# The new tokens' 64-row tile multiplied in float32 with the raw weights

## The reference, cut to what matters

```python
z = gelu(h @ w_in); u, v = split(z)                    # layer 0: 1024 -> 2 x 2048, v is normed and mixed over positions
a = h @ w_in; c_q, c_kv, k_r = split(a)                # layer 1: 1024 -> 384 + 256 + 32, each part normed
q  = (c_q  @ w_uq ).reshape(S, 16, 64 + 32)            # 384 -> 16 heads x 96
kv = (c_kv @ w_ukv).reshape(S, 16, 64 + 64)            # 256 -> 16 heads x (64 key + 64 value columns)
```

## Time and profile before

| | |
|---|---|
| median of 3 runs | 1471.11 us (1470.96 to 1471.82) |
| the profiled execution | 1471.75 us, its span 1469.9 us |
| PE / PEld (weight loads) busy | 1459.4 us (99%) / 1377.7 us (94%) |
| DVE / ACT / POOL busy | 827.2 / 618.6 / 703.2 us |
| matmul records | 10556 |
| granted TensorE clock | 1.00 |
| DMA | 120.33 MB, mean 82 GB/s |

### The profile page before, as it was taken

How to read it: one execution, slowest core, us unless ns; L and a number is a source line. 1 busy time by engine, 2 the same in 40 slices (tenths; PEclk the granted TensorE clock), 3 DMA queues, 4 the chain that set the end, 5 groups by cost and what they waited for, 6 DMA issues and landing times.

```text
span 1469.9 us, 29054 instructions
## 1 busy us (share of the span) xinstructions
PE 1459.4 (99%) x10556; PEld 1377.7 (94%) x10556; DVE 827.2 (56%) x1499; ACT 618.6 (42%) x1234; POOL 703.2 (48%) x474
## 2 busy tenths in 40 slices
PE   9999999999999999999999999999999999999998
PEld 7889999999999999999997778787999999999998
DVE  6006716755654635636778676867556536356365
ACT  5323201123533434435637585766135344344352
POOL 7554455443363453543776052452433644535434
PEclk9999999999999999999999999999999999999999
DMA  7322232231133131231343110101221331312412
GB/s 236 105 83 72 77 105 80 63 86 58 47 127 101 58 114 57 86 117 55 118 152 89 30 44 15 43 18 39 77 67 44 127 95 66 114 57 86 117 56 93
DMA packets 36385, 120.33 MB, mean 82 GB/s; under 512 B 6040, under 2 KB 6744, under 8 KB 36064
## 3 DMA queue, kind: packets, MB, share of 16 engines
q1 hardware_dynamic: 31456, 109.86, 24.1%
q10 hardware_dynamic: 4864, 9.61, 2.0%
HBM read 115.91 MB, written 3.55 MB: 81 GB/s over the span
## 4 chain that ended last, share of the span: by engine, by line
PE 49%; DVE 2%; issue 1%; ACT 1%; DVEq 0%
PE ps L720 8%; PE ps L722 8%; PE ps L721 8%; PE ps L881 5%; PE ps L883 5%; PE ps L882 5%; PE ps L1159 2%; PE ps L1101 2%; PE ps L978 2%; PE ps L1112 1%; PE ps L1104 1%; PE ps L983 1%; PE ps L1026 1%; PE ps L1073 1%; DVE lat L1541 1%
## 5 line engine op out<-in xcount | busy, mean ns | idle before, releaser
L720 PE MATMUL ps<-h_hi,w_hi 128*128 128x288 f32 x1280 | 380.6, 297 | 0.0
L721 PE MATMUL ps<-h_lo,w_hi 128*128 128x288 f32 x1280 | 377.5, 295 | 0.0
L722 PE MATMUL ps<-h_hi,w_lo 128*128 128x288 f32 x1280 | 376.3, 294 | 0.0
L652 POOL TENSOR_TENSOR w_lo<-raw,w_hi 128x512 fp32r<-128x512 f32 x128 | 172.0, 1354 | 213.5 <-ACT w_hi L1879 213.3
L881 PE MATMUL ps<-op_hi,w_hi 128*128 128x288 f32 x896 | 265.5, 296 | 1.1 <-DVE x L1454 1.1
L882 PE MATMUL ps<-op_lo,w_hi 128*128 128x288 f32 x896 | 264.3, 295 | 0.0
L883 PE MATMUL ps<-op_hi,w_lo 128*128 128x288 f32 x896 | 263.4, 294 | 0.0
L722 PEld LDWEIGHTS ps<-h_hi,w_lo 128*128 128x128 f32 x1280 | 241.0, 188 | 0.0
L720 PEld LDWEIGHTS ps<-h_hi,w_hi 128*128 128x128 f32 x1280 | 239.8, 187 | 1.2
L721 PEld LDWEIGHTS ps<-h_lo,w_hi 128*128 128x128 f32 x1280 | 240.3, 188 | 0.0
L636 POOL TENSOR_TENSOR w_lo<-raw,w_hi 128x1024 fp32r<-128x1024 f32 x60 | 144.3, 2411 | 183.7 <-ACT w_hi L1871 183.7
(11 more groups left out here) (211 smaller groups left out, 2730.9 us busy)
## 6 DMA issues: line engine op xcount, KB each, us to landing
raw<-stream SPq DMA_DIRECT2D x206, 512.0 KB, 3.6
out_x<-x ACTq DMA_DIRECT2D x8, 288.0 KB, 2.5
x<-xt SPq DMA_DIRECT2D x4, 288.0 KB, 5.9
x<-xt ACTq DMA_DIRECT2D x4, 288.0 KB, 9.1
raw<-stream ACTq DMA_DIRECT2D x2, 512.0 KB, 7.0
b_bc<-bs ACTq DMA_DIRECT2D x2, 512.0 KB, 7.0
cache_raw<-cache_ct ACTq DMA_DIRECT2D x1, 1024.0 KB, 6.5
v_out<-sgu_grow ACTq DMA_DIRECT2D x1, 512.0 KB, 4.7
```

What stands on the lines that cost most here:

```text
L652: nc.gpsimd.tensor_tensor(block_of(w_lo, b), factor(i, b), block_of(w_hi, b).bitcast(F32), ALU.subtract).then_inc(split_lo, 1)
L720: nc.tensor.matmul(out, l_hi, r_hi, start=first, stop=False)
L721: nc.tensor.matmul(out, l_hi, r_lo, start=False, stop=False)
L722: return nc.tensor.matmul(out, l_lo, r_hi, start=False, stop=last)
```

## The change

Tile 4 of the gating values, the latents and the queries, and the last key tile, are multiplied in float32: one instruction with the float32 activations as stationary operand and the raw weight unit as streamed operand, in place of `three` or `packed`. The other tiles are unchanged. With it:

- `h_new` (DVE, 8 small products x times gain, one per k behind each `low_part`), `h_new2` (POOL, one product of 8 x 64 elements behind the first MLP, which waits for the last x tile and comes before the `split` loop), `cq_new` and `c_new` (ACT, one copy each in `take_latents`) hold the float32 activations of the 64 rows.
- PE waits for `first_new` in chunk 0 and for `new_set` at tile 4 of the first unit of each latent chunk.
- A raw slot is now read by PE until the unit is used, so `plain` waits for `unit_done` of the unit too before it reloads the slot, in the gating values, the latents and the head groups.
- `h_pair`, `packed`, `copy_low_half` and `fold_samples` go, with their semaphores.

```diff
-            def plain(first, end, lows):
+            def plain(first, end, lows, done=None):
+
                 for unit in range(first, end):
                     sp.wait_ge(split_lo, unit - first + lows + 1)
+                    if done is not None:
+                        sp.wait_ge(unit_done, unit - first + done + 1)
                     sp.dma_start(raw[:, unit % SLOTS, :], stream[unit]).then_inc(raw_loaded[unit % SLOTS], 16)
...
-            plain(SLOTS, U_MLP0 + SLOTS, 0)
+            plain(SLOTS, U_SGU + SLOTS, 0, 0)
+            plain(U_SGU + SLOTS, U_MLP0 + SLOTS, U_SGU)
...
-            plain(U_IN + SLOTS, U_GRP + 2 * SLOTS, L_IN)
+            plain(U_IN + SLOTS, U_GRP + SLOTS, L_IN, D_IN)
...
-            plain(U_GRP + 2 * SLOTS, U_MLP1 + SLOTS, L_IN + U_GRP + SLOTS - U_IN)
+            plain(U_GRP + SLOTS, U_O + SLOTS, L_IN + U_GRP - U_IN, D_GRP)
+            plain(U_O + SLOTS, U_MLP1 + SLOTS, L_IN + U_O - U_IN)
...
+            pool.wait_ge(gains_loaded, 16)
+            pool.wait_ge(tile_read, F_O + 2)
+            nc.gpsimd.tensor_tensor(h_new2[:], x[:, :, SEQ:T], gains_sb[:, 2, :].unsqueeze(2).broadcast_to([P, KD, DEC]),
+                                    ALU.mult).then_inc(new_set, 1)
...
-                            if pack and t == NT - 1:
-                                last = packed(ps[:, bank_of(parity, t), 0:width], k, w_hi[:, j, w], w_lo[:, j, w],
-                                              k == 0, k == KD - 1)
+                            if t == NT - 1:
+                                if chunk >= 4 and j == 0:
+                                    pe.wait_ge(new_set, 1)
+                                elif chunk == 0:
+                                    pe.wait_ge(first_new, k + 1)
+                                last = nc.tensor.matmul(ps[0:DEC, bank_of(parity, t), 0:width],
+                                                        (h_new2 if chunk >= 4 else h_new)[:, k, :], raw[:, j, w],
+                                                        start=(k == 0), stop=(k == KD - 1))
                                 continue
...
-                        for t in range(NT):
+                        for t in range(NT - 1):
                             last = nc.tensor.matmul(ps[0:ROWS[t], bank_of(0, t), 0:512], l[:, k, cols(t)], r[:, j, w],
                                                     start=(k == 0 and n == 0), stop=False)
+                    pe.wait_ge(first_new, k + 1)
+                    last = nc.tensor.matmul(ps[0:DEC, bank_of(0, NT - 1), 0:512], h_new[:, k, :], raw[:, j, w],
+                                            start=(k == 0), stop=False)
...
+                        if t == NT - 1:
+                            last = nc.tensor.matmul(ps[0:DEC, q_bank(t, first), 0:HG * QK], cq_new[:, k, :],
+                                                    raw[:, k, 0:HG * QK], start=(k == 0), stop=(k == 2))
+                            continue
...
+                        if j == KT_N - 1:
+                            last = nc.tensor.matmul(ps[0:r, key_bank(j), 0:width], c_new[:, k, :], raw[:, 3, w],
+                                                    start=(k == 0), stop=(k == 1))
+                            continue
...
+                nc.vector.tensor_scalar(h_new[:, k, :], x[:, k, SEQ:T], gains_sb[:, 0, k:k + 1], None,
+                                        ALU.mult).then_inc(first_new, 1)
...
+                    if L % NT == NT - 1:
+                        nc.scalar.copy((cq_new if L < NT else c_new)[:],
+                                       ps[:, latent_bank(L), col:col + n_k * P].rearrange(
+                                           "p (k c) -> p k c", k=n_k)[:, :, 0:r])
```

More of the change, by code:

```diff
@@ L226, in build_trunk @@
         hid_lo = place("hid_lo", [P, KD, T], F32R, b_at + 4 * KD * T)
-        h_pair = place("h_pair", [P, KD, 2 * DEC], F32R, b_at)
+        h_new = place("h_new", [P, KD, DEC], F32, b_at)
         lat = place("lat", [P, NT, QL + KL + ROPE], F32, b_at)
@@ L231, in build_trunk @@
         krr = place("krr", [P, NT, QK], F32, b_at + 4 * (NT + 1) * LAT)
+        h_new2 = place("h_new2", [P, KD, DEC], F32, b_at + 4 * (NT + 1) * LAT + 4 * NT * QK)
+        assert 4 * (NT + 1) * LAT + 4 * NT * QK + 4 * KD * DEC <= 8 * KD * T
         v_at = region(4 * NT * DS)
@@ L246, in build_trunk @@
         cqT_lo = place("cqT_lo", [P, 3, T], F32R, v_at + 16 * KEYS + 12 * T)
+        cq_new = place("cq_new", [P, 3, DEC], F32, v_at + 16 * KEYS + 24 * T)
+        c_new = place("c_new", [P, 2, DEC], F32, v_at + 16 * KEYS + 24 * T + 12 * DEC)
+        assert 16 * KEYS + 24 * T + 20 * DEC <= 4 * NT * DS and 2 * op_bytes + 32 * TH <= 8 * KD * T + 16 * KEYS + 24 * T
         s_at = region(4 * KT_N * HG * VD)
@@ L353, in build_trunk @@
         tok_read = sem_of("tok_read")
-        pair_set = sem_of("pair_set")
-        fold_set = sem_of("fold_set")
-        folded = sem_of("folded")
+        first_new = sem_of("first_new")
+        new_set = sem_of("new_set")
         v_set = sem_of("v_set")
@@ L764, in norm_spread @@
                 last.then_inc(rms_spread, 1)
[L766 to L770, removed]
             def token_chunk(chunk, parity, first_unit, width, between=None, h_count=None, tiles=None,
-                            halves_apart=False, pack=False):
+                            halves_apart=False):
                 for j in range(2 if h_count == 0 else 0, 4):
@@ L834, in _ @@
             pe.wait_ge(var_set, 2)
-            pe.wait_ge(pair_set, 2)
             def spread_first():
@@ L841, in _ @@
             for c in range(1, 4):
-                token_chunk(c, c % 2, 4 * c, 512, pack=True, between={2: spread_first} if c == 3 else None)
+                token_chunk(c, c % 2, 4 * c, 512, between={2: spread_first} if c == 3 else None)
             pe.wait_ge(rms_bc_set, 2)
@@ L1224, in norm_diagonal @@
                 last.then_inc(diag_set, 1)
[L1226 to L1229, removed]
             def clear_sums():
@@ L1286, in _ @@
             norm_diagonal(0)
-            for c in range(1, 4):
-                fold_samples(c - 1, v[0:DEC, NT - 1, c * 512:(c + 1) * 512], bank_of(c, NT - 1))
             dve.wait_ge(const_loaded, 16 * CONSTS)
@@ L1755, in _ @@
             nc.scalar.activation(junk[:, 0:1], ones[:, 0:1], ACT.Square)
-            def copy_low_half(bank, width):
-                nc.scalar.copy(mixed[0:DEC, 0:width], ps[DEC:2 * DEC, bank, 0:width]).then_inc(fold_set, 1)
             def load_half(half):
@@ L1805, in _ @@
             load_half(0)
[L1806 to L1809, removed]
             norm_root(0)
@@ L1824, in _ @@
                     vc = v[0:r, t, c * 512:(c + 1) * 512]
[L1825 to L1829, removed]
+                    nc.scalar.activation(vc, ps[0:r, bank_of(parity, t), :], ACT.Gelu,
                                          scale=rms_tok[0:r, t:t + 1]).then_inc(tok_read, 1)
```

## The result

The changed kernel takes 1508.65 us (median of 4 runs, 1506.99 to 1510.05), the kernel before 1471.36 us beside it: ratio 1.025, 95% interval 1.024 to 1.026. That is 37.3 us slower where 30.2 were predicted, and 0.65 us above the range. The profiled execution took 1510.05 us with a span of 1508.2 us, 38.3 us more than the span of before. It is the slowest of the four runs: PE's mean granted clock was 0.996 in two of them (1510.05 and 1508.4 us) and 0.998 in the other two (1508.9 and 1506.99 us).

A forecast was written before the change was run, and what follows sets the result against it. PE, busy 99% of the span, was taken as the bound. Products 15.4, change-overs 13.3 and the `new_set` stall 1.5 made 30.2 us: 1502.0 us profiled, 1501.3 by the median; range 1487 to 1508 us.

The forecast's parts named there:

- What a product costs: On PE, a 64-row float32 product costs 0.86 us at 512 columns, 0.64 at 384, 0.48 at 288.
- Reading (b): A product runs its two records in a row, 0.86 us; two products in different array halves run together.
- R1: Rival: both records of a product run at once, 0.43 us at 512 columns; +4.7 us, 1475.8 us; chance 0.12.
- R2: Rival: both records at once and change-overs hidden in the float32r stream; -8.6 us, 1462.5 us; chance 0.03.
- The change-over: On PE, each stretch of 64-column float32 products costs 0.36 us, 35 stretches; with the key tiles +13.3 us.
- R3: Rival: records in a row, but change-overs cost nothing; +15.4 + 1.5 us, 1488.0 us; chance 0.06.
- The table: Dearer products in gating, latents, queries and last key: together +15.4 us, of which gating chunks 1 to 3 +9.6.
- `first_new`: Chunk 0: DVE's eight small products before the squares are hidden by DVE's 3.03 us standing; nothing, up to 0.5 us.
- `new_set`: PE waits for POOL's `h_new2` at tile 4 of the first latent unit: 1.5 us, bounds 1.0 and 2.0.
- the waits that were filled: Head group 0: longer products may fill some 0.5 us of PE's 1.6 us stall before L1026; left in the range.
- The late reload: Units ready 7.2 us after their slot's last use, hidden by PE's three units in hand; at worst 1 us once.

The follow-up runs named there:

- e5: e2 with the two tile 4 products of a unit in gating chunks 1 to 3 written to different PSUM partition halves, then added: 1490.94 us, ratio 1.0137.
- e4: e2 with tile 4 of two units multiplied in one stretch (chunks 0 to 5), 14 change-overs fewer: 1496.07 us, ratio 1.017.
- e2: e1 with the latents' `h_new2` also made by ACT, k by k, instead of POOL's one product: 1497.58 us, ratio 1.0175.
- e1: The changed kernel with the eight `h_new` products of the start on ACT instead of DVE: 1500.93 us, ratio 1.020.
- e3: The kernel before with only the changed, later reload of the raw slots, no float32 product: 1476.21 us, ratio 1.003.
- e6: e2 with tile 4 of gating chunks 1 to 3 back to packed float32r products, with copy and fold: 1487.56 us, ratio 1.0106.
- e8: e6 with the same two waits on POOL as e7 (the hold): 1482.76 us, ratio 1.0077.
- e7: e3 with POOL held: low parts of units 19 and 123 wait for DVE's first `vn` products and its latents: 1471.48 us, ratio 1.000.

## Why the prediction was wrong, point by point

**What a product costs** was right. Reading (b), two records in a row of 0.43 us, stands in the loads of the kernel after, and e5 shows that it is the missing partner. R1 and R2 fall with it. R1 rested on a start in program order; read by (b), the pairs of the earlier trace rows are products of two heads side by side. So the second head's first product starts 0.01 us behind the first head's first (807.63 and 807.62), ahead of the first head's second (808.53), which stands before it in the program.

**The change-over** was right: 0.34 us measured directly in the kernel after, 0.34 and 0.32 by taking 14 of them away (e4), 0.36 predicted. R3 falls. The table and the change-overs were 28.7 us in the prediction; e2 has 26 us left.

**`first_new`, the step that failed.** The prediction put it so: "DVE's eight small products lie in front of the squares. DVE then stood 3.03 us waiting for PE, and PE comes to that point later still: hidden." It took the eight for nearly nothing; they took 15.4 us of DVE, 10.4 us net on the squares' start. And it took 3.03 us of standing behind the squares for slack in front of them. That was 1.7 us, and 2.8 more because PE itself came later: 10.4 - 1.7 - 2.8 = 5.9. The cost was 9.1 us of the gating by the traces of the kernel after and e1 (the stall of 5.9 and the half clock behind it are 8.8), 7.7 by the medians. Without it, e1 is 0.4 us from the forecast of 1501.3. That is partly luck: `new_set` and the reload cost more than was forecast, the waits that were filled gave more.

The trace of before had the warning. DVE and POOL of the kernel before, in order of time:

```profile
17.87 2.95 DVE L1239 SCALAR_TENSOR_TENSOR h_lo<-x,gains_sb,h_hi 128x576 fp32r<-128x576 f32 x1
...
17.43 2.78 POOL L613 TENSOR_TENSOR w_lo<-raw,w_hi 128x1024 fp32r<-128x1024 f32 x1
20.18 1.56 POOL L611 TENSOR_SCALAR w_hi<-raw 128x1024 fp32r<-128x1024 f32 x1
```

`h_lo`, which alone takes 0.8 us, takes 2.95 there and ends behind POOL's `w_lo`. POOL's next `w_hi` takes 1.56 us instead of the 1.05 of an undisturbed one. The two engines already held each other up in this stretch. An operation added to DVE there costs what is left of POOL's, however small it is itself. The Trainium skill states the rule, in SBUF — State Buffer, section Who interferes with whom: DVE and GpSimd share a port pair as an exclusive lock, and whoever issues second is blocked for the other's whole instruction, for `tensor_scalar` in a two-port mode and for DVE operations with two inputs in SBUF against GpSimd ones that read it. These traces agree (2.37 us for 64 elements, 3.35 for two `vn` products), and so does ACT's 0.33.

**`new_set`** was right in kind and place. The stall was 1.8 us in place of 1.5, since `h_new2` took 1.55 us and not 1.2. The 1.7 us of half clock behind it in the kernel after had not been counted; e1, with the same stall and no half clock, is 1.6 us shorter in the latents. e2 got 2.3 us back there, 3.35 by the medians.

**The late reload, the second step that failed.** "PE has three units in hand ... Hidden." That PE does not wait for weights was right, and e3 has no such wait. But the sum asked only whether the weights come in time, not where POOL's work goes when it is shifted, and what it falls on there: 4.5 us in e3. In the kernel after itself little of it shows: 0.8 us before L961, in head group 0, and no wait for `vn`. There the fold of tile 4 is gone, and DVE begins `vn` at 143.93, 3.2 us before PE's product that reads it (147.10) and ahead of POOL's next `w_hi` (144.68); in the kernel before it was 1.0 us (120.08 and 121.11). The wait came back in e5 and e6, which have the fold, and with 0.8 us in e4, which has not. So the late reload cost the changed kernel about 1 us (the hold gave 1.1 in e8's head groups), and stood ready for the next edit.

**The sum, redone for the kernel after:** products 15.4, 35 stretches at 0.34 and the key tiles 12.6, first stall and its clock 8.8, `new_set` and its clock 3.5, waits for `h_lo` and `lat` 1.3: 41.6 us, against 38.3 measured between the spans. By stage: gating 26.4 (26.8 measured), latents 7.8 (7.0), head groups 7.4 (6.2), feature tiles 0 (-1.2), start 0 (-0.5). Most of the gap is waits that the kernel before has and the kernel after has not. In the feature tiles and the first MLP those of before are

```profile
PE ps L881 <- DVE x L1454: 1.1, 2, 0.8
PE ps L862 <- DVE vn L1305: 0.3, 1, 0.3
```

and the kernel after waits 0.2 us for x and not for `vn`: that is the 1.2 us. In the latents the kernel before loses 0.7 us at the transposes of L946 (at 762.0 and 767.1), seen against e7, which has the same products there; the kernel after runs through them in rhythm. In the head groups the 1.6 us of the earlier trace rows, two waits and not one as the prediction read them, are 0.9. That leaves 0.5 us in the head groups, which are open, and the start, which differs by more from trace to trace.

## What to carry to other kernels

Before putting even a 64-element operation on DVE or POOL, look at what the other of the two does in that stretch: where neighbours there already take two or three times their usual time, the small one will too, and ACT is the place for it. Slack is counted up to the instruction that waits, not up to the next idle gap of the engine that got the work. And when a transfer or a split is moved, ask not only who needs its result, but also on whose instructions its work now lands.

## What was not expected of the hardware

- A DVE product of 128 x 64 elements took up to 2.37 us beside POOL's `w_lo`. On ACT, beside the same work of POOL, it took 0.33 us (e1).
- PE's granted clock fell to half (1.2 GHz) for 3.4 or 6.8 us behind stalls of 1.8 to 5.9 us in the kernel after, e3 and e6. It did not in the traces of e1, which has the same 1.8 us stall, and of e5 with its 2.7 us, nor in every run of e3. Which of the stalls are followed by it the runs leave open.
- Two float32 products with 64 stationary columns, one after the other in the program, run beside each other if they write different halves of the PSUM partitions: four records of 512 columns in 0.86 us, 1.72 in the same half.
